# A two-block transformer on one core: neighbourhood attention moved inside the projection tiles of its own gate, queries and keys

## The reference, cut to what matters

```python
h = rmsnorm(x, norm_g[l])                     # 512 tokens, 1024 wide
proj = h @ w_in[l]                            # q_a k_a v_a g_a | q_b k_b v_b g_b, 512 columns each
out_a = neighborhood_attention(q_a, k_a, v_a, na_rpb[l])   # 8 heads of 64, window 8 rows x 16 columns
out_b = diff_attention(q_b, k_b, v_b, ...)                 # 4 heads
y = concatenate([out_a * silu(g_a), out_b * silu(g_b)])
x = x + y @ w_out[l]
```

## Time and profile before

| | us |
|---|---|
| median of 3 runs (lowest, highest) | 921.02 (920.84, 921.49) |
| the profiled execution, its own time | 922.06 |
| its span, first to last instruction | 920.2 |
| PE busy | 888.8 (97%) |
| DVE busy | 577.1 (63%) |
| ACT busy | 449.8 (49%) |
| POOL busy | 110.9 (12%) |

### The profile page before, as it was taken

One profiled execution on the slowest core, in us unless ns is written; L12 is line 12 of the kernel. 1 busy time (PEld: TensorE's weight loads), 2 busy tenths in 40 slices (PEclk: granted clock), 3 DMA queues, 4 the chain that ended last, 5 costly groups with the idle time before them and its releaser, 6 DMA issues.

```text
span 920.2 us, 14682 instructions
## 1 busy us (share of the span) xinstructions
PE 888.8 (97%) x5733; PEld 709.1 (77%) x5733; DVE 577.1 (63%) x1170; ACT 449.8 (49%) x956; POOL 110.9 (12%) x137
## 2 busy tenths in 40 slices
PE   3999999999999999999999999999999999999996
PEld 1579888775677778888888886788888888887785
DVE  5899797989787464667372447245576645335633
ACT  4724323476786334566435339234466633536731
POOL 1001111013200010000010017200000001003702
PEclk9999999999999999999999999999999999999999
DMA  9736646255200333222124234122422232334103
GB/s 382 324 97 137 179 149 185 104 162 204 92 3 1 115 109 115 91 88 92 48 93 154 96 94 133 43 92 92 137 67 88 73 135 92 97 95 130 47 24 92
DMA packets 34678, 104.69 MB, mean 114 GB/s; under 512 B 14961, under 2 KB 14961, under 8 KB 32178
## 3 DMA queue, kind: packets, MB, share of 16 engines
q1 hardware_dynamic: 28098, 85.77, 28.0%
q0 software_dynamic: 3856, 15.73, 5.3%
q10 hardware_dynamic: 2656, 2.26, 1.0%
HBM read 98.37 MB, written 4.19 MB: 111 GB/s over the span
## 4 chain that ended last, share of the span: by engine, by line
PE 90%; DVE 4%; ACT 3%; issue 1%; DMA 1%; SPq 0%; POOL 0%; POOLq 0%; DVEq 0%; ACTq 0%
PE bank L1092 83%; PE bank L1452 2%; PE bank L1432 2%; PE bank L1598 2%; DMA ring<-in_w_ada 1%; PE bank L1513 1%; DVE arena L1727 1%; ACT ring L999 0%; PE bank L1503 0%; ACT w_hi L938 0%; ACT arena L771 0%; ACT soft L1006 0%; DVE xn_t L2238 0%; DVE w_lo L2213 0%; DVE ring_lo L2262 0%
## 5 line engine op out<-in xcount | busy, mean ns | idle before, releaser
L2213 DVE TENSOR_TENSOR w_lo<-ring,w_hi 128x1024 fp32r<-128x1024 f32 x80 | 97.7, 1224 | 88.2 <-ACT w_hi L938 85.6
L1092 PE MATMUL bank<-hT_hi,w_hi 128*128 128x512 f32 x320 | 128.1, 400 | 0.0
L1092 PE MATMUL bank<-w_hi,hT_hi 128*128 128x512 f32 x320 | 127.1, 397 | 0.3 <-DVE hT_lo L2256 0.3
L1092 PE MATMUL bank<-hT_lo,w_hi 128*128 128x512 f32 x320 | 124.9, 390 | 0.0
L1092 PE MATMUL bank<-w_lo,hT_hi 128*128 128x512 f32 x320 | 124.9, 390 | 0.0
L1092 PE MATMUL bank<-hT_hi,w_lo 128*128 128x512 f32 x320 | 124.8, 390 | 0.0
L1092 PE MATMUL bank<-w_hi,hT_lo 128*128 128x512 f32 x320 | 124.6, 389 | 0.0
L938 ACT ACTIVATE w_hi<-ring 128x1024 fp32r<-128x1024 f32 x80 | 84.4, 1057 | 14.1 <-PE bank L1092 13.8
L1092 PEld LDWEIGHTS bank<-hT_hi,w_hi 128*128 128x128 f32 x320 | 60.1, 188 | 16.5 <-issue 4.4
L1092 PEld LDWEIGHTS bank<-w_hi,hT_hi 128*128 128x128 f32 x320 | 60.1, 188 | 14.6 <-issue 3.0
L1092 PEld LDWEIGHTS bank<-hT_lo,w_hi 128*128 128x128 f32 x320 | 60.1, 188 | 13.1
(11 more groups left out here) (328 smaller groups left out, 1738.0 us busy)
## 6 DMA issues: line engine op xcount, KB each, us to landing
ring<-in_w_units SPq DMA_DIRECT2D x80, 512.0 KB, 3.7
ring<-in_w_ada SPq DMA_DIRECT2D x4, 2048.0 KB, 10.5
bias_ring<-in_na_bias POOLq DMA_DIRECT2D x6, 1024.0 KB, 5.2
ring<-in_w_out SPq DMA_DIRECT2D x2, 2048.0 KB, 9.0
bias_ring<-in_t_bias POOLq DMA_DIRECT2D x8, 448.0 KB, 3.7
x_t<-in_x SPq DMA_DIRECT2D x4, 512.0 KB, 6.1
arena<-in_w_ada SPq DMA_DIRECT2D x1, 2048.0 KB, 20.2
arena<-in_w_ada SPq DMA_DIRECT2D x2, 1024.0 KB, 23.0
```

Of the source, the lines that this page charges most:

```text
L1092: return pe.matmul(out, lhsT, rhs, start=first, stop=last)
L2213: dve.tensor_tensor(w_lo[:, u % 4], raw_w[:, u % 4], w_hi[:, u % 4].bitcast(fp32), SUB).then_inc(S["w_split"], 1)
```

## The change

It takes the tail apart and puts the 16 units, two by two, inside the projection tiles. `ga`, `qa` and `ka` are no longer three groups but 12 tiles in the mixed order of `NA_TILES`. A pair of units is scored in the middle of tile x (x in `NA_AT` = 3, 4, 6 to 11), its first unit is turned in the middle of tile x+1 and its second behind that tile, and both are weighed in the middle of tile x+2. What is left of pairs 6 and 7 after tile 11 stands between the first steps of the output tiles. `na_score` waits for the takes of the pair before last and writes two units into one pair of banks; `na_turn` has one bank instead of two; `na_weigh` waits for the `na_out` of the pair before it instead of the one before that. The projection tiles take two banks in turn.

`mix_T` moves to tiles (4,3) to (5,2). Its split (`mixT_hi`, `mixT_lo`) moves to tiles 8 to 11, as the last thing that ACT and DVE do in each, and its result goes into the q and k tiles that are spent. The gate is evacuated by one tanh on ACT and one operation on DVE per tile; before, ACT did two operations and DVE one more behind the group. `na_out` writes once; the high part is made by ACT (`na_hi`, 128x512, four a layer) and the low part by POOL (`na_lo`, now 128x512, four a layer) after the last `mixT_lo`. The output projection waits for each slice's low part.

```diff
-KINDS = ("vb", "qkb", "qkb", "gb", "va", "ga", "qa", "ka", "o0", "o1")
+KINDS = ("vb", "qkb", "qkb", "gb", "va", "gqka", "gqka", "gqka", "o0", "o1")
 COL0 = {"qa": 0, "ka": 512, "va": 1024, "ga": 1536, "qb": 2048, "kb": 2560, "vb": 3072, "gb": 3584}
 BY_TOKENS = ("vb", "gb", "va", "o0", "o1")
 OUT_ORDER = [4, 5, 6, 7, 0, 1, 2, 3]
+NA_TILES = (("ga", 0), ("qa", 0), ("ka", 0), ("ga", 1), ("qa", 1), ("ka", 1), ("qa", 2), ("ka", 2), ("qa", 3), ("ka", 3), ("ga", 2), ("ga", 3))
...
-        EARLY = {1: (0,), 2: (1, 2)}
-        N_EARLY = 3
+        NA_AT = [3, 4, 6, 7, 8, 9, 10, 11]
         HK_AT = 7
-        MIX_AT = (4, 6, 8, 10)
-        MIX_TURNS = [(5, 1), (5, 3), (6, 1), (6, 3)]
-        MIX_LAG = 2
-        NA_LAG = 3
+        MIX_AT = (8, 9, 10, 11)
+        MIX_TURNS = [(4, 3), (5, 0), (5, 1), (5, 2)]
...
+            return bank[2 + t % 2 if p >= PT_B2 and g in (1, 2, 3, 5, 6, 7) else p % 4]
+
+        def na_scores(m, e):
+
+            return bank[4 + m // 2 % 2 * 2 + e][:, m % 2 * KW:(m % 2 + 1) * KW]
+
+        def na_rows(g):
+
+            return bank[1][:, g % 2 * 256:(g % 2 + 1) * 256]
+
+        def na_pair(x, lag):
+
+            return NA_AT.index(x - lag) if x - lag in NA_AT else None
+
+        def mix_parts(m):
+
+            hi, lo = (q_hi, q_lo) if m % 2 == 0 else (k_hi, k_lo)
+            return hi[:, m // 2, :], lo[:, m // 2, :]
...
-            def na_lo(l, g):
-                pool.wait_ge(S["na_out"], N_NA // 2 * l + g + 1)
-                cols_ = slice(g % 2 * 256, g % 2 * 256 + 256)
-                pool.tensor_tensor(hT_lo[:, g // 2, cols_], y2[:, g // 2, cols_], hT_hi[:, g // 2, cols_].bitcast(fp32), SUB)\
-                    .then_inc(S["na_lo"], 1)
+            def na_lo(l, p):
+
+                pool.wait_ge(S["mixed_hi"], 8 * l + 4 + p + 1)
+                pool.tensor_tensor(hT_lo[:, p, :], y2[:, p, 0:512], hT_hi[:, p, :].bitcast(fp32), SUB).then_inc(S["mixed_lo"], 1)
...
-                    if m >= 6 and m % 2 == 0:
-                        na_lo(l, m // 2 - 3)
-                for g in range(N_NA // 2 - 3, N_NA // 2):
-                    na_lo(l, g)
+                pool.wait_ge(S["mixed_lo"], 8 * l + 4)
+                for p in range(4):
+                    na_lo(l, p)
...
+            def mixT_hi(l, m):
+
+                act.wait_ge(S["mixT_moved"], 4 * l + m + 1)
+                act.activation(cut(mix_parts(m)[0], i=NT, t=P), mixT[m], ACT.Copy).then_inc(S["mixed_hi"], 1)
+
+            def na_hi(l, p):
+
+                act.wait_ge(S["na_out"], N_NA // 2 * l + 2 * p + 2)
+                act.activation(hT_hi[:, p, :], y2[:, p, 0:512], ACT.Copy).then_inc(S["mixed_hi"], 1)
...
+                    what, p = NA_TILES[4 * (g - 5) + t]
+                    if what == "ga":
+                        act.activation(y2[:, p, 0:512], src[:, :], ACT.Tanh, scale=0.5).then_inc(S["half_evac"], 1)
+                    else:
+                        act.activation((k_hi if what == "ka" else q_hi)[:, p, :], src[:, :], ACT.Copy, scale=1.0 if what == "ka" else SCALE)\
+                            .then_inc(S["half_evac"], 1)
...
-                            if KINDS[g] == "ka" and t - 1 in EARLY:
-                                for m in EARLY[t - 1]:
-                                    na_exp(l, m)
+                            tile = 4 * (g - 5) + t
+                            turned, scored = na_pair(tile, 1), na_pair(tile, 0)
+                            if not half and turned is not None:
+                                na_move(l, 2 * turned)
+                            if not half and scored is not None:
+                                na_exp(l, 2 * scored)
+                                na_exp(l, 2 * scored + 1)
                             evacuate(l, g, t)
                             if half and n >= 0:
                                 da_slot(l, n + 1)
+                            if not half and turned is not None:
+                                na_move(l, 2 * turned + 1)
                             if KINDS[g] not in BY_TOKENS:
                                 split_hi(u + t)
+                            if not half and tile in MIX_AT:
+                                mixT_hi(l, MIX_AT.index(tile))
...
-                        for j in range(N_EARLY, N_NA + NA_LAG):
-                            na_move(l, j - NA_LAG)
-                            if j < N_NA:
-                                na_exp(l, j)
-                            if j in MIX_AT:
-                                m = MIX_AT.index(j)
-                                mixT_hi(l, m, 4 + m, mixT[m])
+                        na_hi(l, 0)
+                        na_hi(l, 1)
+                        na_move(l, N_NA - 2)
+                        na_hi(l, 2)
+                        na_move(l, N_NA - 1)
+                        na_hi(l, 3)
...
+                    rows_ = mix_parts(k - 4) if g >= 8 and k >= 4 else (hT_hi[:, k, :], hT_lo[:, k, :])
...
-                if M >= 2:
-                    pe.wait_ge(S["na_taken"], 2 * M - 2)
+                if M >= 4:
+                    pe.wait_ge(S["na_taken"], 4 * (M // 2) - 4)
...
-                if m % 2 == 0 and M >= 4:
-                    pe.wait_ge(S["na_out"], M // 2 - 1)
+                if m % 2 == 0 and M >= 2:
+                    pe.wait_ge(S["na_out"], M // 2)
...
+                    def na_amid(tile):
+
+                        turned, weighed, scored = (na_pair(tile, lag) for lag in (1, 2, 0))
+                        if turned is not None:
+                            na_turn(l, 2 * turned)
+                        if weighed is not None:
+                            na_weigh(l, 2 * weighed)
+                            na_weigh(l, 2 * weighed + 1)
+                        if scored is not None:
+                            pe.wait_ge(S["mixT_moved"], 4 * (l + 1))
+                            pe.wait_ge(S["proj_evac"], pt2(l, 5) + NA_TILES.index(("ka", scored // 2)) + 1)
+                            na_score(l, 2 * scored)
+                            na_score(l, 2 * scored + 1)
...
-                            in_turn = g == 1 and t >= 2 or g in (2, 3) or g == 4 and t < 2
+                            in_turn = g in (1, 5) and t >= 2 or g in (2, 3, 6, 7) or g == 4 and t < 2
...
+                            turned = na_pair(4 * (g - 5) + t, 1)
+                            if not half and turned is not None:
+                                na_turn(l, 2 * turned + 1)
                     if not half:
 
                         def out_rows(t, b, steps):
 
-                            pe.wait_ge(S["na_taken"], 2 * (N_NA * (l + 1) - 1))
-                            pe.wait_ge(S["mixT_lo"], 4 * (l + 1))
                             return tile_tok(bank[b], l, 8, t, OUT_ORDER, None, steps)
 
-                        for j in range(N_EARLY, N_NA + NA_LAG + 1):
-                            if j < N_NA:
-                                na_score(l, j)
-                            if j <= N_EARLY + 1:
-                                pe.wait_ge(S["proj_evac"], pt2(l, 8) - 1 + j - N_EARLY)
-                            if j < N_NA + NA_LAG:
-                                na_turn(l, j - NA_LAG)
-                            if j > N_EARLY:
-                                na_weigh(l, j - NA_LAG - 1)
-                            if j == N_NA:
-                                out_rows(0, 6, range(0, 4))
+                        pe.wait_ge(S["na_taken"], 2 * N_NA * (l + 1))
+                        pe.wait_ge(S["mixed_lo"], 8 * l + 4)
+                        out_rows(0, 6, range(0, 4))
+                        na_turn(l, N_NA - 2)
+                        na_weigh(l, N_NA - 4)
+                        na_weigh(l, N_NA - 3)
+                        na_turn(l, N_NA - 1)
                         out_rows(1, 7, range(0, 4))
-                pe.wait_ge(S["na_taken"], 2 * N_NA * (l + 1))
-                pe.wait_ge(S["na_lo"], N_NA // 2 * (l + 1))
-                for t in range(2):
-                    out_rows(t, 6 + t, range(4, KD)).then_inc(S["wo_done"], 1)
+                        na_weigh(l, N_NA - 2)
+                        na_weigh(l, N_NA - 1)
+                for p in range(4):
+                    pe.wait_ge(S["mixed_lo"], 8 * l + 4 + p + 1)
+                    ins = out_rows(0, 6, range(4 + p, 5 + p))
+                ins.then_inc(S["wo_done"], 1)
+                out_rows(1, 7, range(4, KD)).then_inc(S["wo_done"], 1)
...
-                    dve.wait_ge(S["na_scored"], k + 1)
+                    dve.wait_ge(S["na_scored"], 2 * N_NA * l + 4 * (m // 2 + 1))
...
-                o = na_bank(2 * g)
+                dve.wait_ge(S["proj_evac"], pt2(l, 5) + NA_TILES.index(("ga", g // 2)) + 1)
                 y = y2[:, g // 2, g % 2 * 256:g % 2 * 256 + 256]
-                dve.tensor_tensor(hT_hi[:, g // 2, g % 2 * 256:g % 2 * 256 + 256], o[:, 0:256], y, MUL)
-                dve.tensor_tensor(y, o[:, 0:256], y, MUL).then_inc(S["na_out"], 1)
```

(54 more changed lines are left out.)

63 lines of the change are left out of this document (18 added, 45 removed).

## The result

| | before | after |
|---|---|---|
| median (lowest to highest, 4 runs each) | 921.25 (920.84 to 922.06) | 929.81 (929.10 to 930.57) |
| the profiled execution, its own time | 922.06 | 929.10 |
| its span | 920.2 | 927.3 |
| PE busy | 888.8 (97%) | 887.6 (96%) |
| mean granted clock of the span | 0.999 | 0.992 |

The change makes the kernel slower by 8.56 us, a ratio of 1.0092 [1.0074, 1.0109]. The forecast was 924.0, its range 921.0 to 928.0: the sign was right, the size was not, and the range missed it.

The account below looks back on a forecast made before the run. PE's own order of work was taken to set the time. Per layer -3.89 of work and +5.41 of new waits gave +1.52, twice +3.04; on the median 921.02 that made 924.0 us, range 921.0 to 928.0.

Parts of the forecast that it names:

- PE's work without waits: One layer's rebuilt stretch, matmuls and shape changes added up: 103.90 us, 3.89 under the 107.79 of before.
- wait behind tile 11: PE, ahead of output tile 0, waits for the fourth mixT_lo: 4.10 us each layer.
- wait in tile 6: PE's weighing waits for the na_out of the pair before, with no turn ahead: 0.54 us a layer.
- waits in tiles 9, 10, 11: PE's weighings wait for the na_out of the pair before: 0.10 us each, 0.30 a layer.
- wait for the last slice: At the stage's end PE waits for POOL's na_lo of the last slice: 0.47 us a layer.
- the clock: PE's clock in the stage should stay at 1.00 of full, so the sum held nothing for it.
- the sum above has none: The summed forecast of 924.0 us included no fall of the clock in PE's long wait.
- The rule on the clock: TensorE idle long enough falls to 1.2 GHz until sustained work, so the long wait might cost more than its length.
- The price of a fall: Clock rival: matmuls behind the long wait run slow, 1.4 to 3.4 us each time, 925.4 to 930.8; chance 0.17.
- faster: Rival: PE hides shape changes beside big matmuls wholly, 3.2 us off a layer, 917.6; chance 0.08.
- The shapes give more and the waits less: Rival: waits of 3.6 instead of 5.4 us a layer, 920.4, or 922.2 with half of it; chance 0.24.
- the late supply: Rival: a transfer or weight split comes late in the mixed tiles, 1 us or more a layer, 926 to 928; chance 0.05.

Follow-up runs that it names:

- e1: Changed kernel with 16 big matmuls that nobody reads put ahead of PE's wait behind tile 11, once a layer; 925.34 us, ratio 1.0040.
- e2: Changed kernel with, in tile 11 alone, the last mixT_hi ahead of split_hi on ACT and mixT_lo ahead of split_lo on DVE; 922.85 us, ratio 1.0016.
- e3: Changed kernel with the split of mixT moved from tiles 8 to 11 to tiles 5 to 8 (one line); 917.30 us, ratio 0.9953.
- e5: Changed kernel with mixT's split at tiles 5 to 8, na_out ahead of split_lo, and visits ordered weighing, score, weighing, score; 917.15 us, ratio 0.9952.
- e7: e2 with 8 big matmuls that nobody reads in PE's wait; 921.13 us, ratio 0.9995.
- e8: e2 with 4 big matmuls that nobody reads in PE's wait; 920.95 us, ratio 0.9996.
- e9: Changed kernel with 8 big matmuls that nobody reads ahead of PE's wait behind tile 11; 926.32 us, ratio 1.0055.

## Why the prediction was wrong

| term, layer 0 | forecast | measured |
|---|---|---|
| PE's work without waits | 103.90 | 103.78 |
| wait behind tile 11 | 4.10 | 4.17 |
| wait in tile 6 | 0.54 | 0.67 |
| waits in tiles 9, 10, 11 | 0.30 | 0.66 |
| wait for the last slice | 0.47 | 0.45 |
| the clock | 0 | 1.50 |
| stage | 109.31 | 111.23 |

Measured: 4.17 is 577.21 less 572.68 less the turn's 0.36; 1.50 is that of e1; PE's work is what remains. In layer 1 the clock took 2.60, and 112.21 less that is 109.61.

**The step that failed** is "the sum above has none" and the chance of 0.17 behind it: the clock was put at nothing, and it cost 4.47 us. The rule on the clock stood in the text, its condition (idle time of 3.9 us) was forecast to 0.1 us, and it was weighed against "No stretch of this trace shows such a fall". That was weak, as inside the stages no idle piece was longer than 0.72, so their clock of 1.00 said nothing about 3.9. It was also wrong: PE is idle for long at both ends of the trace of before, and the low clock can be read at both.

At the start PE waits 14.38 us for its first matmul. The record of the clock in this trace begins only at 19.95 us, and the view shows 1.00 for all that lies ahead of it. The matmuls show half of that. A block of four of the same shape follows the last after 0.85, and behind 19.95 after 0.45:

```profile
15.20 1.11 PE L1092 MATMUL bank<-ring,csl_pad 128*32 128x512 f32 x4
16.05 1.11 PE L1092 MATMUL bank<-ring,csl_pad 128*32 128x512 f32 x4
...
21.38 0.64 PE L1092 MATMUL bank<-ring,csl_pad 128*32 128x512 f32 x4
21.83 0.61 PE L1092 MATMUL bank<-ring,csl_pad 128*32 128x512 f32 x4
```

The transposes between them start 0.21 apart from 18.43 to 19.71 and 0.11 apart from 20.19 on. In the trace of the changed kernel the record begins at 18.67, and there the step changes in the middle of a run of transposes: they start at 18.26, 18.48, 18.69, 18.80 and 18.91.

At the end of the trace of before, PE's last matmul starts at 912.62 and ends at 913.01:

```profile
912.62:917.00 4.38, 0.39 (x2) 0.00 (x0) 1.44 (x2) 1.45 (x3) 0.73 (x2) 1.00 0.44 120
...
917.50:918.00 0.50, 0.00 (x0) 0.00 (x0) 0.00 (x0) 0.00 (x0) 0.00 (x0) 0.66 0.92 188
918.00:920.20 2.20, 0.00 (x0) 0.00 (x0) 0.00 (x0) 0.00 (x0) 0.00 (x0) 0.50 0.59 196
```

The clock falls at 917.66 (0.66 is the mean of 0.16 us at 1.00 and 0.34 at 0.50), 4.65 after PE's last work. Neither stretch says that 3.9 us are enough, but both show the low clock in this kernel where PE had long been idle, and a chance of 0.17 resting on "no row shows a fall" had no ground left. The Trainium skill, TensorE: Matmul & The Clock Gate (Part 1, "HAM oscillation"), warns that an idle wait between bursts starts the next burst cold, each time. The trace agrees in layer 1, where the clock is at 0.50 when PE goes on; in layer 0 the burst starts at full clock and the fall comes 1.25 us into it.

**The price of a fall**, 1.4 to 3.4, was taken from 16 transposes at 3.26 against 1.91, put down to the low clock, and a factor of one to two and a half. The low clock is there, but it makes only part of the 1.35: the first eight transposes start within 1.52 (18.19 to 19.71), and seven steps of 0.11 are 0.76, so it costs some 0.76. Most of the rest is two gaps, 0.34 from 19.71 and 0.38 from 20.41, where a step is 0.11 elsewhere. The factor had no row. So that 1.50 and 2.60 fall into the range, and 929.81 into the 925.4 to 930.8 of this rival, is in part luck. The forecast's upper end, 928.0, left out the case of two falls, which is what came: 925.34 and two falls of 4.47 in all.

**The waits.** The chain behind tile 11 came as laid out; ACT, DVE and POOL in the changed kernel:

```profile
572.88 0.60 ACT L1028 ACTIVATE y<-bank 128x512 f32<-128x512 f32 x1 [0.23 <-PE bank L1113]
573.38 0.59 ACT L1019 ACTIVATE soft<-bank 128x512 f32<-128x512 f32 x1
573.86 1.06 ACT L951 ACTIVATE w_hi<-ring 128x1024 fp32r<-128x1024 f32 x1
...
574.95 1.22 DVE L2245 TENSOR_TENSOR w_lo<-ring,w_hi 128x1024 fp32r<-128x1024 f32 x1 [0.74 <-ACT w_hi L951]
...
576.09 0.42 DVE L2360 TENSOR_TENSOR y<-bank,y 128x256 f32<-128x256 f32 x1
576.42 0.68 DVE L2251 TENSOR_TENSOR k_lo<-y,k_hi 128x512 fp32r<-128x512 f32 x1
577.18 1.28 POOL L613 TENSOR_TENSOR hT_lo<-y,hT_hi 128x512 fp32r<-128x512 f32 x1 [2.60 <-DVE k_lo L2251]
```

With E at 572.68, `split_hi` starts at E+1.18 (forecast 1.17), `split_lo` at E+2.27 (2.26), `mixT_lo` at E+3.74 (3.73), and PE goes at E+4.53 (4.45). e2 and e3 confirm the cause: the place of `mixT_hi` and `mixT_lo` in the queues. POOL takes 1.28 for the step that had no row, near the 1.32 taken from the earlier trace rows. What was small was mis-sized: in tiles 9 to 11 the turn ahead of the weighing takes 0.75, not 0.63.

```profile
558.35 0.60 PE L1620 MATMUL bank<-cons,ring 128*128 128x128 f32 x4
559.10 0.66 PE L1113 MATMUL bank<-soft,v 128*64 128x128 f32 x8 [0.15 <-DVE y L2360]
559.56 0.64 PE L1113 MATMUL bank<-soft,xn_t 128*64 128x128 f32 x8
560.13 0.38 PE L1113 MATMUL bank<-k_hi,q_hi 64*128 64x256 f32 x2
...
561.03 0.50 PE L1113 MATMUL bank<-hT_hi,w_hi 128*128 128x512 f32 x1
```

There 0.10 was the difference of two sums of four terms. The same rows show the visit at 1.03 and 0.90, as forecast. With tile 6 these errors make 0.49 a layer, 1.0 of the 1.34 between the forecast's 924.0 and e1's 925.34.

**The shapes.** PE's work was right to 0.12. A full tile takes 8.79 from closing turn to closing turn (555.13 to 563.92), which is 8.57 without its wait of 0.22, against a forecast of 8.58. That two units pay once for a change of shape is shown by e5, for the change between the two small shapes. No run varies the change between small and big matmuls, but the rows show its price: the first big matmul behind a score or a weighing is followed after 0.34 (561.03 to 561.37), not 0.23, and PE's work came as forecast with these prices. So the rival "faster", in which they are nothing, is out. "The shapes give more and the waits less" is out by the waits, 5.95 a layer in the table instead of 3.6. No wait for a transfer appears in the stage's list: the late supply did not come.

## What to carry to other kernels

When an edit makes an engine wait, ask which step is last in the queue that it waits for and whether that step could stand one tile earlier: here one line of order was worth 12.5 us, more than the 8.75 that the change gives in its best version. When an edit leaves PE idle for 2 us or more in one piece, count a fall of the clock as likely and price it beside the wait (1.5 to 2.6 us a time here). Look for the clock's behaviour where the trace has long idle time, its start and its end too, before saying that it shows none, and read it from the distance of equal matmuls as well as from the clock column.

## What the runs showed of the hardware

- Each low stretch seen between matmuls lasted 3.4 or 6.8 us. One of 3.4 cost 1.50, 1.57 and 1.51 us by the timelines (layer 0 of the changed kernel, e2, e9) and 1.7 to 2.1 by the medians (e2 against e7 and e8). The one of 6.8 cost 2.60; PE was still idle for its first 1.15.
- A fall came 5.18 and 2.77 us after PE's last work ahead of the wait in the changed kernel, 2.43 in e2, 3.14 in e9, and 4.65 behind the last matmul of before. It can come when PE is already back at work, as in layer 0 above, so that a fall stands some matmuls behind its cause.
- Idle pieces of 3.92 us were followed by a fall in both layers, pieces of 2.0 in one of two (e2, e9, one profile each), those of 1.05 and less in none. Why one piece of 2.0 brings a fall and its twin does not stays open.
- At the kernel's start TensorE works at the low clock, though the view shows 1.00. The record of the clock begins at 19.95 us in before and at 18.67, 20.10, 18.71 and 18.33 in the changed kernel, e1, e2 and e9, and in each the transposes go from 0.21 to 0.11 apart there.
